# Two heads' half-array matmuls side by side, and compression with the token blocks stationary

## The reference

```python
def hybrid_layer(x, ...):
    proj = rms_norm(x, norm_mix) @ w_in
    y_nsa = nsa_mixer(...)   # 8 heads of 64 in 2 groups: compressed, selected, window attention
    y_sb  = stick_breaking_mixer(sb_q, sb_k, sb_v)          # 8 heads of 64
    y_gla = gla_mixer(...)                                  # 4 heads, keys of 64, values of 128
    y_fox = forgetting_mixer(fox_q, fox_k, fox_v, fox_f)    # 8 heads of 64
    mixed = sum over the branches of sigmoid(gates) * (y @ w_branch)
    x = x + mixed @ w_out
    return x + square(relu(rms_norm(x, norm_ff) @ w_ff1)) @ w_ff2

# inside nsa_mixer: 15 overlapping blocks of 32 tokens, stride 16, per group
def compress(t, pe, w1, w2):
    blk = t[:, cmp_idx] + pe[:, None, :]          # [15 blocks, 32 tokens * 64]
    return gelu(blk @ w1) @ w2                    # hidden width 256

# inside stick_breaking_mixer, z the scaled scores of 256 queries with 256 keys
sp = where(valid, softplus(z), 0)
later = reverse_cumsum(sp) - sp
a = where(valid, exp(log_sigmoid(z) - later), 0)
```

## Time and profile before

| what | us |
|---|---|
| runs shown, median of 3 | 2196.72 |
| the profiled execution, whole | 2188.58 |
| its span, first to last instruction | 2186.8 |
| mean granted clock of TensorE | 0.926 |

### The profile page before, as it was taken

The page is one execution under the profiler, slowest core; times in us unless marked ns, Lnnn a source line. Parts: engine busy times, 40 slices in busy tenths (PEclk is TensorE's granted clock), DMA queues, the critical chain, the costliest instruction groups (busy, mean ns, idle before and its releaser), DMA issues.

```text
span 2186.8 us, 29173 instructions
## 1 busy us (share of the span) xinstructions
PE 1926.1 (88%) x11788; PEld 1516.2 (69%) x11788; DVE 852.2 (39%) x1433; ACT 766.8 (35%) x1099; POOL 119.4 (5%) x112
## 2 busy tenths in 40 slices
PE   6977799999987878999897799977899998797997
PEld 4854344444443767788797699876788888787986
DVE  2043211111111324333466666432343336575653
ACT  1140122212221315473445334331456444433432
POOL 0000000000000003202100000000140030000000
PEclk9988899999999858999998899987699999899999
DMA  5423499999997332232243434442223232343452
GB/s 217 185 89 152 187 427 428 427 427 428 427 428 325 142 116 78 78 116 109 85 155 116 154 147 175 187 155 82 79 111 116 78 127 107 114 154 147 171 196 100
DMA packets 30885, 412.33 MB, mean 189 GB/s; under 512 B 3600, under 2 KB 5040, under 8 KB 5808
## 3 DMA queue, kind: packets, MB, share of 16 engines
q1 hardware_dynamic: 30768, 410.68, 47.2%
HBM read 408.84 MB, written 1.84 MB: 188 GB/s over the span
## 4 chain that ended last, share of the span: by engine, by line
issue 85%; PE 7%; POOL 5%; DVE 1%; DMA 1%; ACT 0%; SPq 0%; POOLq 0%; DVEq 0%; ACTq 0%
POOL work_mem L1710 5%; PE bank L740 3%; PE bank L748 3%; DMA work_mem<-in_const 1%; PE bank L835 0%; PE bank L772 0%; PE bank L817 0%; POOL small L1718 0%; DVE ht_mem L1749 0%; PE bank L810 0%; PE bank L774 0%; PE bank L775 0%; DVE work_mem L1869 0%; POOL small L1691 0%; DVE work_mem L1886 0%
## 5 line engine op out<-in xcount | busy, mean ns | idle before, releaser
L1505 ACT ACTIVATE w_hi<-wring 128x2048 fp32r<-128x2048 f32 x88 | 168.5, 1915 | 298.5 <-PE bank L1048 167.0
L2075 DVE TENSOR_TENSOR w_lo<-wring,w_hi 128x2048 fp32r<-128x2048 f32 x88 | 201.3, 2292 | 183.3 <-ACT w_hi L1505 183.3
L1047 PE MATMUL bank<-mixed_hi,w_hi_early 128*128 128x256 f32 x960 | 244.1, 291 | 6.9 <-DVE mixed_lo L2083 4.3
L1505 ACT ACTIVATE w_hi_early<-wring 128x2048 fp32r<-128x2048 f32 x80 | 152.9, 1911 | 267.0 <-PE bank L1048 177.4
L1048 PE MATMUL bank<-mixed_lo,w_hi_early 128*128 128x256 f32 x960 | 238.8, 286 | 0.0
L2075 DVE TENSOR_TENSOR w_lo<-wring,w_hi_early 128x2048 fp32r<-128x2048 f32 x80 | 183.2, 2290 | 123.8 <-ACT w_hi_early L1505 123.8
L1052 PE MATMUL bank<-mixed_hi,w_lo 128*128 128x256 f32 x1472 | 208.0, 284 | 0.0
L1047 PEld LDWEIGHTS bank<-mixed_hi,w_hi_early 128*128 128x128 f32 x960 | 186.7, 194 | 12.5 <-issue 6.4
L1052 PEld LDWEIGHTS bank<-mixed_hi,w_lo 128*128 128x128 f32 x1472 | 191.4, 193 | 0.0
L1048 PEld LDWEIGHTS bank<-mixed_lo,w_hi_early 128*128 128x128 f32 x960 | 186.9, 195 | 0.0
L966 PE MATMUL bank<-wring,gates_mem 128*64 128x512 f32 x768 | 171.7, 604 | 13.0 <-DMA wring<-in_w 13.0
(11 more groups left out here) (418 smaller groups left out, 3314.8 us busy)
## 6 DMA issues: line engine op xcount, KB each, us to landing
wring<-in_w SPq DMA_DIRECT2D x160, 2048.0 KB, 8.7
work_mem<-in_w SPq DMA_DIRECT2D x32, 2048.0 KB, 17.3
cst<-in_const SPq DMA_DIRECT2D x1, 1273.0 KB, 7.6
prm<-in_prm SPq DMA_DIRECT2D x3, 381.0 KB, 9.3
x_mem<-in_x SPq DMA_DIRECT2D x1, 1024.0 KB, 4.9
out_x<-x_mem SPq DMA_DIRECT2D x1, 1024.0 KB, 3.9
rel_skew<-work_mem SPq DMA_DIRECT2D x1, 768.0 KB, 3.5
work_mem<-in_prm SPq DMA_DIRECT2D x1, 512.0 KB, 12.4
```

Of the source, the lines that this page charges most:

```text
L1047: pe.matmul(out, w[0][:, k, cols], x[0][:, k, :], start=(k == 0), stop=False)
L1505: act.activation(hi, w, ACT.Copy).then_inc(hi_ready, 1)
L2075: dve.tensor_tensor(lo, w, hi, ALU.subtract).then_inc(lo_ready, 1)
```

## The change

1. **Order of the steps.** The lists go by pairs of heads: two scores, then fillers, then the later steps of an earlier pair. NSA keeps one filler per two scores, and its `turn` follows two pairs later. Stick-breaking and forgetting attention have two fillers in a row per pair, and `again` or `turn` follow one pair later. The NSA jobs are renumbered so that a pair is the two groups of one branch.
2. **Pairs on PE.** The matmuls on the lower and the upper half of the rows (scores, the score part of `again`, the GLA levels, the compressed scores) or of the columns (values) are issued in turn, into two banks or two halves of a bank. In `again`, the five whole-array matmuls of each head follow behind the four half-array ones.
3. **Compression.** The token blocks are stationary (31 columns: 15 of each group and one unused) and the weights move (256 columns); the 16 steps of the contraction are spread over four column groups of 32 (q = 0 to 3), so a bank holds four partial sums. ACT copies the four of them into SBUF (`hid_parts`, cleared by DVE at the start of each layer), and a matmul with the constant 0/1 matrix `winsum` adds them up and turns them into the layout of before (`hsum`).

```diff
 def sb_steps():                      # fox_steps the same, with "turn" for "again"
+    out, fill, pairs = [], list(SB_FILL), SB_N // 2
+    for p in range(pairs + SB_LAG + 1):          # SB_LAG = FOX_LAG = 1 pair, NSA_LAG = 2 pairs
+        if p < pairs:
+            out += [("score", 2 * p), ("score", 2 * p + 1)]
+        out += [("fill", f) for f in fill[0:2]]
+        del fill[0:2]
+        done = p - SB_LAG
+        if 0 <= done < pairs:
+            out += [("again", 2 * done), ("again", 2 * done + 1)]
+        if done > 0:
+            out.append(("value", done - 1))
...
+        def scores_of_two(jobs, q, k, turn):     # NSA
+            for j in jobs:
+                free(j, turn)
+            for r, j in enumerate(jobs):
+                pe.matmul(psum[j.bank][:, 0:P], q[r][:, 0:P], k[r][:, 0:P], start=True, stop=True)
+            for r, j in enumerate(jobs):
+                pe.matmul(psum[j.bank][:, P:384], q[r][:, P:S], k[r][:, 0:S], start=True,
+                          stop=True).then_inc(bank_full[j.bank], 1)
...
-                for half in range(2):
-                    for k in range(16):
-                        win = dup[:, 2 * n + k // 8, :].rearrange("p (g c s) -> p g c s", g=2, s=CMP_STRIDE)
-                        mm = pe.matmul(psum[j.bank][:, half * 30:half * 30 + 30].rearrange("p (g c) -> p g c", g=2),
-                                       w[:, k, half * P:(half + 1) * P],
-                                       win[:, :, k // 8:k // 8 + N_CMP, 2 * (k % 8)], start=(k == 0), stop=(k == 15))
+                for step in range(4):
+                    for q in range(4):
+                        k = 4 * step + q
+                        win = dup[:, 2 * n + k // 8, :].rearrange("p (c s) -> p c s", s=CMP_STRIDE)
+                        mm = pe.matmul(psum[j.bank][32 * q:32 * q + 2 * N_CMP + 1, 0:CMP_HIDDEN],
+                                       win[:, k // 8:k // 8 + 2 * N_CMP + 1, 2 * (k % 8)], w[:, k, :],
+                                       start=(step == 0), stop=(step == 3))
+                mm.then_inc(bank_full[j.bank], 1)
+            for n, j in enumerate(layer["hsum"]):
+                parts_read = layer["hid"][n]
+                pe.wait_ge(bank_read[parts_read.bank], parts_read.count(l))
+                free(j, l)
+                for half in range(2):
+                    mm = pe.matmul(psum[j.bank][:, half * 2 * N_CMP:(half + 1) * 2 * N_CMP],
+                                   hid_parts[:, n, half * P:(half + 1) * P], C("winsum"), start=True, stop=True)
                 mm.then_inc(bank_full[j.bank], 1)
...
             for n, j in enumerate(layer["hid"]):         # on ACT
+                full(j, l)
+                for q in range(4):
+                    rows = slice(32 * q, 32 * q + 2 * N_CMP + 1)
+                    ins = act.activation(hid_parts[rows, n, :], psum[j.bank][rows, 0:CMP_HIDDEN], ACT.Copy)
+                ins.then_inc(bank_read[j.bank], 1)
...
             norm_x(2 * l + 4, xn_a)                      # on DVE
+            dve.memset(flat2(hid_parts), 0.0).then_inc(hid_parts_clear, 1)
             split_lo(0)
...
+            def stick_again(jobs, n):
+                for j in jobs:
+                    free(j, l)
+                for j, (q, k) in zip(jobs, two_heads(n)):
+                    pe.matmul(psum[j.bank][:, S:384], k[:, P:S], q[:, P:S], start=True, stop=False, skip_group_check=True)
+                for j, (q, k) in zip(jobs, two_heads(n)):
+                    pe.matmul(psum[j.bank][:, 0:S], k[:, 0:P], q, start=False, stop=False, skip_group_check=True)
+                for r, j in enumerate(jobs):
+                    ... five whole-array matmuls on bank j: sufneg, negstrict, sufneg, negtriu, negstrict
...
                 elif kind == "again":
-                    pe.wait_ge(sb_ready, 8 * l + n + 1)
-                    free(j, l)
-                    stick(j, n, False).then_inc(bank_full[j.bank], 1)
+                    if n % 2 == 0:
+                        pe.wait_ge(sb_ready, 8 * l + n + 2)
+                        stick_again([j, layer["sb", kind, n + 1][0]], n)
```

More of the change, by code:

```diff
@@ L185, in __getitem__, with last_in_bank @@
         return self.jobs[name]
-def last_in_bank(jobs, but=None):
-    last = {}
+def last_in_bank(jobs, but=()):
+    last, apart = {}, [j.bank for j in but]
     for j in jobs:
-        if but is None or j.bank != but.bank:
+        if j.bank not in apart:
             if j.bank not in last or last[j.bank].use < j.use:
@@ L258 @@
 GLA_FILL = [("gates", j) for j in range(6, 16)]
-NSA_N, NSA_LAG = 16, 3
-SB_N, SB_LAG = 8, 3
-FOX_N, FOX_LAG = 8, 3
+NSA_N, NSA_LAG = 16, 2
+SB_N, SB_LAG = 8, 1
+FOX_N, FOX_LAG = 8, 1
 def nsa_steps():
-    out, fill = [], list(NSA_FILL)
-    for n in range(NSA_N + NSA_LAG + 2):
-        if n < NSA_N:
-            out.append(("score", n))
-        if 0 <= n - NSA_LAG < NSA_N:
-            out.append(("turn", n - NSA_LAG))
-        if n % 2 == 1 and fill:
+    out, fill, pairs = [], list(NSA_FILL), NSA_N // 2
+    for p in range(pairs + NSA_LAG + 1):
+        if p < pairs:
+            out += [("score", 2 * p), ("score", 2 * p + 1)]
+        done = p - NSA_LAG
+        if 0 <= done < pairs:
+            out += [("turn", 2 * done), ("turn", 2 * done + 1)]
+        if fill:
@@ L273, in nsa_steps @@
             out.append(("fill", fill.pop(0)))
-        k = n - NSA_LAG - 1
-        if k >= 0 and k % 4 == 3:
-            out.append(("value", k // 4))
+        if done > 0 and done % 2 == 0:
+            out.append(("value", done // 2 - 1))
     return out + [("fill", f) for f in fill]
 def sb_steps():
-    out, fill = [], list(SB_FILL)
-    for n in range(SB_N + SB_LAG + 2):
-        if n < SB_N:
-            out.append(("score", n))
-        if fill:
-            out.append(("fill", fill.pop(0)))
-        if 0 <= n - SB_LAG < SB_N:
-            out.append(("again", n - SB_LAG))
-        k = n - SB_LAG - 1
-        if k >= 0 and k % 2 == 1:
-            out.append(("value", k // 2))
+    out, fill, pairs = [], list(SB_FILL), SB_N // 2
@@ L292, in sb_steps @@
+    for p in range(pairs + SB_LAG + 1):
+        if p < pairs:
+            out += [("score", 2 * p), ("score", 2 * p + 1)]
+        out += [("fill", f) for f in fill[0:2]]
+        del fill[0:2]
+        done = p - SB_LAG
+        if 0 <= done < pairs:
+            out += [("again", 2 * done), ("again", 2 * done + 1)]
+        if done > 0:
+            out.append(("value", done - 1))
     return out + [("fill", f) for f in fill]
 def fox_steps():
[L296 to L306 removed]
+    out, fill, pairs = [], list(FOX_FILL), FOX_N // 2
@@ L307, in fox_steps @@
+    for p in range(pairs + FOX_LAG + 1):
+        if p < pairs:
+            out += [("score", 2 * p), ("score", 2 * p + 1)]
+        out += [("fill", f) for f in fill[0:2]]
+        del fill[0:2]
+        done = p - FOX_LAG
+        if 0 <= done < pairs:
+            out += [("turn", 2 * done), ("turn", 2 * done + 1)]
+        if done > 0:
+            out.append(("value", done - 1))
     return out + [("fill", f) for f in fill]
@@ L1025, in heads_out @@
             free(j, turn)
-            for r in range(2):
-                rows = slice(HD * r, HD * r + HD)
-                pe.matmul(psum[j.bank][rows, 0:S], lhs[r][0], rhs[r][:, 0:S], start=True, stop=False)
-                mm = pe.matmul(psum[j.bank][rows, P:S], lhs[r][1], rhs[r][:, S:384], start=False, stop=True)
+            halves = [psum[j.bank][HD * r:HD * r + HD, :] for r in range(2)]
+            for r, out in enumerate(halves):
+                pe.matmul(out[:, 0:S], lhs[r][0], rhs[r][:, 0:S], start=True, stop=False)
+            for r, out in enumerate(halves):
+                mm = pe.matmul(out[:, P:S], lhs[r][1], rhs[r][:, S:384], start=False, stop=True)
             mm.then_inc(bank_full[j.bank], 1)
@@ L1199, in stick @@
[L1199 to L1213 removed]
+            in_sbuf(layer["sb_q"] + layer["sb_k"] + layer["sb_v"], l, *(layer["sb", "score", n][0] for n in range(2)))
```

151 lines of the change are left out of this document (83 added, 68 removed).

## The result

| what | before | changed |
|---|---|---|
| median of the runs, us | 2197.2 (4 runs, 2195.5 to 2198.6) | 2122.4 (4 runs, 2121.7 to 2125.4) |
| profiled execution, us | 2188.58 | 2122.42 |
| span, us | 2186.8 | 2120.6 |
| mean granted clock | 0.926 | 0.920 |

The ratio is 0.9664, 95% interval 0.9653 to 0.9676: faster by 74.8 us at the medians and by 66.2 us from profiled execution to profiled execution. The forecast was 2140 us, the range 2110 to 2180.

The account below looks back on a forecast made before the run. PE, busy for 88% of the span, was taken as the bound. Terms of -28.4 us a layer, twice -56.8, took the profiled 2188.6 to 2131.8; with 8.1 added for the median, 2140 us, range 2110 to 2180.

Parts of the forecast that it names:

- PE's own part, -12.3: Stick-breaking: paired scores -3.4, paired `again` -7.6 and the old 1.3 us wait gone, -12.3 us a layer.
- (a): Stick-breaking: the two low parts are not late, DVE or ACT get through earlier; 2085 us, chance 0.08.
- the two terms 20.8 + 6.8: Stick-breaking, per layer: PE waits for the second fillers' low parts, +20.8 us; clock lost through these waits, +6.8 us.
- (b): Compression: column groups run two at a time, not four; 2152 us, chance 0.15.
- (c): Compression: column groups run one at a time, each load waiting for the matmul ahead; 2180 us, chance 0.04.
- (d): NSA, stick-breaking, forgetting attention, GLA: row pairs alternating record by record do not overlap; 2180 us, chance 0.03.
- (e): Stick-breaking: waits of 5 us keep TensorE at 1.2 GHz for the whole stage; 2220 us, chance 0.06.
- I put them at the low level, since it fell there before: Compression: the 32 records of values run at 1.2 GHz and take 3.4 us, against 1.7 us for keys.
- My term: Compressed scores: 32 records lose half, but ACT's exponential waited only 0.56 us and table loads take over; -0.6 us.
- my -1.7: End of NSA: `turn` two pairs late lets a filler cover most of PE's idle time there; -1.7 us.
- +0.8 for the late reciprocal of head 7: End of forgetting attention: the reciprocal stands on DVE behind a value product's copy, POOL's two scalings follow; +0.8 us.
- The added 8.1 us: Whole kernel: the median of the runs lies 8.1 us above the profiled execution, turning 2131.8 into 2139.9 us.

Follow-up runs that it names:

- low-part-first kernel: Changed kernel with DVE's low part of each stick-breaking pair's second filler moved ahead of the two softplus steps: 2066.25 us, ratio 0.9416.
- one-group kernel: Changed kernel with all 16 compression steps in column group 0 and one ACT copy instead of four: 2135.14 us, ratio 0.973.
- head-by-head kernel: Changed kernel with one head's two matmuls issued before the other's in NSA, stick-breaking and forgetting scores and `again`: 2121.19 us, ratio 0.9663.
- compression-only kernel: Kernel before the change with the new compression alone, steps and pairs as before: 2156.37 us, ratio 0.9834.

## Why the prediction was right, and where it was off

Term by term for layer 1, from start to start on PE. The time of a stage includes the idle time at its end.

| stretch | forecast | measured |
|---|---|---|
| layer's start to compression | +0.5 | +1.3 |
| compression to its second product | -17.5 | -19.5 |
| to the start of NSA | -0.6 | -2.1 |
| NSA | -17.4 | -16.3 |
| stick-breaking | +15.3 | +15.1 |
| forgetting attention | -5.2 | -7.7 |
| GLA | -3.5 | -3.0 |
| rest | 0 | -0.5 |
| sum | -28.4 | -32.7 |

Layer 2 gains 34.2 us. Its stages do not all repeat those of layer 1 to a few tenths, as was said ahead of the prediction: NSA took 88.5 us there before the change and 86.3 in layer 1, since the low clock of the compression lasted until 1572.49, 8.4 us into NSA, and it gains 18.0.

**Stick-breaking** was right in each step. PE through with the first filler at 6.87 us (forecast 6.8), ACT with both heads at 8.06 (8.2), DVE's low part at 11.38 (11.6), the waits 4.50, 6.28, 4.52 and 4.61, 19.9 in all (20.8), or 20.9 with what the stops cost besides. The clock took 7.8 us, where I had 6.8 from the short stretch of the earlier trace rows; the stretches here are 6.83 us long, not 3.4, though PE's work fills only 3.7 to 5.0 us of each. PE's own part, -12.3, came out at about -13.5 (68.1 against 81.7). That the sum fits to 0.2 us is partly luck: the last two errors cancel.

**Rivals.** (a), that the low parts are not late, was wrong as a forecast and is what the low-part-first kernel does: -56 us, as the two terms 20.8 + 6.8 taken twice say (55). (b), two column groups at a time, and (c), one at a time, are both excluded by the factor of 3.6. With them falls the rule as I read it in the Trainium skill (page "TensorE: Matmul & The Clock Gate", section "The mechanism"): its sentence on weight loads and row groups doesn't hold for these float32 matmuls, whose four column groups have the same rows. No column groups are needed to see it. In the one-group kernel the loads run beside the matmuls of the same rows, and in the fillers before the change a record on the whole array starts every 0.120 us, each with a load of 0.192 us of its own. Had the groups come one at a time, it would not have been the loads' doing. (d) is excluded by the 0.86 us pair, and by the head-by-head kernel for the weaker claim that the order of the two matters. (e), the low level through the whole stage, did not come: the clock was back at 1.00 after each 6.83 us, with dense work going on.

**Compression: the mis-sized term.** The step "I put them at the low level, since it fell there before" failed. The clock stood at 1.00 in both halves, and fell only at 796.16, so that values took as long as keys. Before that fall PE had short records with idle times of 1.09 and 2.00 us between them, and the level then stayed low for 20.5 us. My figure for ACT's copies was right (1.53 us for four). -19.5 was the bound that I had given for full clock.

**The layer's start.** The low-clock stretch there lasts 20.5 us instead of 13.7 (707.4 to 727.9 against 708.9 to 722.6), in the compression-only kernel too (708.8 to 729.3). I had put the clearing at 0.5; moving it away neither shortened the stretch of low clock (20.5 again) nor the time. In layer 2 this stretch is as long as before (10.24 and 3.41 us), and yet the term is +1.7. There two later low stretches ahead of the compression grew, from 3.4 and 10.2 to 6.8 and 13.7 us. In both layers 6.8 us more lie at the low level, and what adds them stays open.

**To the start of NSA.** My term went by ACT's exponential, which waited only 0.56 us for the compressed scores, and stopped there. The rows that decided are ACT's Ln ahead of it and DVE's list. Before (these rows are not among those ahead), and DVE after:

```profile
822.11 0.72 ACT L1582 ACTIVATE gates_mem<-gates_mem,cst 128x512 f32<-128x512 f32 x1
...
823.42 0.28 DVE L2166 TENSOR_TENSOR work_mem<-bank,cst 128x120 f32<-128x120 f32 x1 [2.30 <-PE bank L1161]
...
824.87 0.42 DVE L2178 TENSOR_SCALAR gates_mem<-gates_mem 128x512 f32<-128x512 f32 x1
825.32 1.27 DVE L2180 TENSOR_TENSOR_SCAN work_mem<-gates_mem 128x256 f32<-128x256 f32 x2
```

```profile
804.87 0.43 DVE L2243 TENSOR_SCALAR gates_mem<-gates_mem 128x512 f32<-128x512 f32 x1 [0.31 <-ACT gates_mem L1645]
```

DVE had GLA's scans behind the compressed scores in its list, and the normalization of the compressed softmax behind the scans. Before, ACT's Ln was done at 822.83 and DVE came to it only at 824.87: 2.0 us were to be gained there, and 0.4 more since the Ln itself now comes earlier. Counted from the second product, DVE is through with the scores 2.8 us earlier, most of it by the pairs (3.59 us of PE and not 6.18). So it came to the scans 0.31 us too early and waited for the Ln, and what stands behind is 2.4 us earlier. NSA starts 2.1 us earlier, since PE's idle time just ahead of it is 1.06 us and not 0.72. So ACT's table loads did take over, as forecast, but in front of DVE's scans and not of the exponential.

**NSA.** Pairs (0.86) and values (2.03) as forecast. The error of 1.1 is what several smaller ones leave. The first pair lies at the low level, in the stretch that began at 796.16, and takes 1.59 us (812.91 to 814.50): +0.7. The filler behind it, at that level until 816.64, costs +0.9. A head's scores cost 0.82 us before and not 0.84, and the pairs 0.86: +0.4. An idle time of 0.68 us is left at the end, where my -1.7 left none: +0.8. Against them stand the last value product, 5.62 us before at a clock of 0.70 and now 2.03, of which I had counted 3.0 (-0.6), and the transposes of two heads, 0.63 us together instead of 0.48 and 0.30 (-1.0 in the stage).

**Forgetting attention.** The pair costs 2.63, not 2.8: another -0.7. I charged +0.8 for the late reciprocal of head 7. The wait is there (1.17 us, released by POOL), but two waits of 0.64 and 0.58 us at the end of the stage before have gone, which I had not set against it. The remaining 1 us is spread over transposes, values and the first records of fillers.

**GLA.** A level takes 1.09 us from start to start instead of 1.64, a gain of 0.55 where I had 0.44 (the 1.71 us of the earlier trace rows is a length, with the time that the last results need to leave the array in it). Eight levels are -4.4. But the low-clock stretch at its start, 6.8 us long as before, now begins 0.6 us before PE resumes (1048.75 against 1049.34) and before the change 3.7 us, so it covers 6.2 us of PE's work instead of 3.2; that takes back 1.4.

**The added 8.1 us.** Nearly half of the error of 17.5 us. The layers come to 2131.8 in terms of the profiled execution, and that of the changed kernel took 2122.4. I then added the distance of before's profiled execution from its median. But the changed kernel's profiled execution lies on its own median (2122.42 and 2122.4). The runs of before other than the profiled one spread from 2190.0 to 2207.3, over all comparisons, those of the changed kernel from 2121.7 to 2125.4: no run shows that such an offset carries over, and here it did not. Whether before's spread comes from its long low-clock stretch in the compression (787.4 to 831.8) was not tried; the compression-only kernel has no such stretch (794.1 to 811.2 in its place), and its four runs still spread over 9 us.

## What to carry to other kernels

When steps are grouped, follow each in-order engine's list and ask what now stands ahead of the thing the busiest engine needs next: a low part that needed nothing from the softplus cost 56 us for standing behind it, and one reordering on an engine that is busy for 40% of the span got them back. Price an idle time of TensorE at the wait plus the clock, and test the two apart by giving it work of no use. A serial chain across three engines is read to its end on all three before its gain is written off, and an offset between a profile and a median is not carried over to another kernel.

One thing was left untried. A table load stands at every change between Exp and Ln, 2.56 of the 4.25 us of a head's softplus. The rows show that this kernel loads a table there, not that the two functions need different ones.

## What the runs showed of the hardware

- Four column groups of 31 columns on the same 128 rows, each record with a weight load of its own, ran side by side: 64 records of 256 columns in 3.84 us, against 13.96 in one group, at the same granted clock (1.00); from step to step 0.216 us for four records or for one.
- Weight loads ran beside matmuls of the same rows and columns: 0.13 us each under records every 0.216 us in one group, 0.192 us each under records every 0.120 us in the fillers before.
- Two heads on different halves of the rows, with two matmuls each, overlap without being alternated: 0.86 us in either order, four records of the second head starting ahead of earlier issued ones of the first. Five matmuls of one column half ahead of five of the other did not (4.03 us, against 2.03 in turn).
- In all eight idle times of 4.5 to 6.3 us of the changed kernel the level fell to 1.2 GHz and was back 6.83 us later, with dense work going on. In the head-by-head kernel the first of them, 4.50 us as well, brought only 3.4 us, from 894.7 to 898.1, when PE was already at work again. With 0.2 to 2.0 us of idle time left in the same places, no low stretch appeared; between the short records behind the compression, idle times of 1.09 and 2.00 us did precede one.
- A filler's record follows the last after 0.213 us at 1.2 GHz and after 0.120 us at 2.4 GHz: the low level makes this work 1.78 times as long, not twice.
